# Input weights of the retention mixer in long runs, the first unit in four transfers, and products of ones at the seam

## The chip, the cores and the metric

One core of one Trainium2 chip runs the whole program. The metric is device microseconds of one execution, the median of several. The core has a matrix engine (PE, its weight loads shown as PEld), a vector engine (DVE), a scalar engine (ACT), GpSimd (POOL) and a sync engine (SP) that issues nearly all transfers here; 16 DMA engines carry them.

## The reference, cut to what matters

Two layers over 256 tokens of width 1024, all in float32. Each layer adds a mixer and then a mixture of experts (32 experts in 4 groups, two chosen per token). The first layer's mixer is attention, the second one's is retention. The work around the change is the end of the first layer's experts and the start of the retention mixer:

```
x = x + hier_moe(rmsnorm(x))              # layer 0, experts
z = rmsnorm(x) @ w_in_o                   # 1024 -> 6144: q, k (4 heads x 256), v, g (4 heads x 512)
q, k, v, g = split(z);  q, k = rope(q), rope(k)
o = rms(retention(q, k, v)) * silu(g)
x = x + o @ w_out_o
x = x + hier_moe(rmsnorm(x))              # layer 1, experts
```

## The kernel before, in words

Weights pass through a ring of 11 slots in SBUF, each 128 partitions by 4096 floats (2 MB, a "unit"). An experts' layer reads 96 units (gate, up and down of 32 experts), each of which lies in DRAM as one run of 16 KB per partition. The last of the 96 comes in two halves. SP issues all unit loads from one program in a fixed order; ahead of a load it waits until the slot's earlier unit is used (`moe_used`, `odd_used`).

The retention mixer reads 16 units in the order `ODD_ORDER`: for the first head qk, v and g, then qk, output weights, v and g of the next heads. `load_odd(j)` issues them. A qk unit is gathered from `w_in_o` by two transfers (q columns, k columns) in runs of 256 floats (1 KB), a v or g unit by one transfer in runs of 512 floats (2 KB); an output unit has longer runs. SP's order at the seam is: qk of head 0 into slot 6, the constants of the mixer (1 MB, `consts_odd`, runs of 8 KB per partition), v of head 0, g of head 0, qk of head 1, then three units of the next experts' layer.

Products with these weights run as three products of rounded parts. ACT writes the high part of a quarter of a unit (`high`, called through `odd_high_of`, L1316), DVE subtracts it to get the low part (`low`, through `odd_low_of`, L1639), and PE waits for the quarter's low part. At the seam ACT alternates: a quarter of the first unit, then two eighths of x (`high_x`, L1506); DVE follows with the low parts (L1639, L1925). ACT waits once for the whole first unit, ahead of its first quarter:

```
here = sum(32 if ODD_ORDER[n][0] == "qk" else 16 for n in range(j % 4, j + 1, 4))
act.wait_ge(odd_here[s_], here)
```

PE's order there is: the last combining products of the experts (`combine_last`, L1050); `first_qk`, 96 products of 256 columns (L1184), eight groups of 12, which needs quarter k // 2 and the low part of eighth k of x; `token_major("v", 0, row_squares)`, 24 products of 512 columns for the first 128 tokens (L657, L660, L661), then `row_squares` (L673) and 24 for the other tokens; `ret_scores` (L1211). `row_squares` takes the sums of squares of x. These are made by ACT (four squares, L1556, behind the four high quarters of v) and added by POOL (`sum_squares`, L627 three times and L628). DVE's order after the first unit is: low parts of v (L1639), the rotation of q and k (L1943, L1944, L1948, L1949, `rotate`), low parts of g, and then the row scales (L1991, L1992) that ACT needs to drain v (L1525). The second score product needs the PSUM bank that the first v occupied.

The routing, the experts and the retention stage are ordered by semaphores alone, nothing in them depends on absolute time.

Of the kernel before, what the change touches and what calls it, by code (L numbers as in the profile page):

```python
# [29 lines left out]
P = 128  # L30
SEQ = 256
TC = SEQ // P
D = 1024
DC = D // P
EPS = 1e-6
Q_LORA, KV_LORA, ROPE, NOPE, VD = 256, 128, 32, 64, 64
HEADS = 8
# [5 lines left out]
RH, RQK, RV = 4, 256, 512  # L43
# [5 lines left out]
UNIT = 4096  # L49
# [72 lines left out]


def build(nc, x_in, w_in_e, ln_q_e, w_uq_e, ln_kv_e, w_ukv_e, w_out_e,
          w_in_o, w_out_o, w_gate, w_up, w_down, ln_f, gains_turned, w_router, b_small, consts, consts_odd, out):
    ctx = ExitStack()
    with ctx:
        def sb(name, shape, dt=F32):
# [2 lines left out]
        def sem(name):  # L131
            return ctx.enter_context(nc.semaphore(name))
# [12 lines left out]
        def at(floats, name, shape, dt=F32):  # L145
            return nc.alloc_sbuf_tensor_at(name, shape, dt, offset=base + 4 * floats)[tuple(slice(None) for _ in shape)]

        ring = at(0, "ring", [P, RING, UNIT])
# [25 lines left out]
        x = at(4 * UNIT + 2048, "x", [P, TC, D])  # L174
# [64 lines left out]
        ones = cut(1)  # L239
        all_ones = ones.broadcast_to([P, P])  # L240
# [29 lines left out]
        gmax, first, sg4, p1 = (rt[:, 2 * k:2 * k + 2] for k in range(4))  # L270
# [18 lines left out]
        wk = [ctx.enter_context(nc.psum_tensor(f"wk{i}", [P, 512], F32)) for i in range(4)]  # L289
# [13 lines left out]
        odd_here = [sem(f"odd_slot{s}_loaded") for s in range(RING)]  # L303
        moe_used = [sem(f"moe{l}_units_used") for l in range(2)]
        odd_used = sem("odd_units_used")
        even_high, even_low = sem("even_high_parts"), sem("even_low_parts")
        odd_high, odd_low = sem("odd_high_parts"), sem("odd_low_parts")
        pe_s = sem("pe_steps")
# [78 lines left out]
        def wide(s):  # L387
            return ring[:, s, :].rearrange("p (c n) -> p c n", c=DC)

        def tall(s):  # L390
            return ring[:, s, :].rearrange("p (c n) -> p c n", c=4)
# [16 lines left out]
        def odd_parts(j):  # L408
            return ODD_HIGH[j % 2], ODD_RAW[j % 4]
# [16 lines left out]
        def last_unit(l, slot):  # L426
            return max(u for u in range(MOE_UNITS) if moe_slot(l, u) == slot)

        def unit_used(u):

            return RING + u + 1 - MOE_UNITS
# [3 lines left out]
        ODD_ORDER = [("qk", 0), ("v", 0), ("g", 0)]  # L435
# [29 lines left out]
        def _(sp):  # L465
# [17 lines left out]
            wo = w_out_e[0].rearrange("(u c p) n -> u p c n", u=2, c=4)  # L483
# [39 lines left out]
                load_expert_part(0, u)  # L523
            n0 = rest_of_experts(0)

            wi = w_in_o[0].rearrange("(c p) n -> p c n", p=P)
            wo2 = w_out_o[0].rearrange("(h c p) n -> h p c n", h=RH, c=4)

            def load_odd(j):
                kind, h = ODD_ORDER[j]  # L530
                s = odd_parts(j)[1]
                if kind == "qk":
                    for m in range(2):
                        sp.dma_start(wide(s)[:, :, m * RQK:(m + 1) * RQK],
                                     wi[:, :, h * RQK + m * RH * RQK:(h + m * RH + 1) * RQK]
                                     ).then_inc(odd_here[s], 16)
                elif kind == "wo":
                    sp.dma_start(tall(s), wo2[h]).then_inc(odd_here[s], 16)
                else:
                    first = 2 * RH * RQK + (RH * RV if kind == "g" else 0)  # L540
                    sp.dma_start(wide(s), wi[:, :, h * RV + first:(h + 1) * RV + first]).then_inc(odd_here[s], 16)

            def moe0_left(slot):
                sp.wait_ge(moe_used[0], n0 * MOE_UNITS + unit_used(last_unit(0, slot)))
# [2 lines left out]
            for j in range(4):  # L547

                moe0_left(odd_parts(j)[1])
                load_odd(j)  # L550
                if j == 0:
                    moe0_left(9)
                    sp.dma_start(odd[:, :], consts_odd).then_inc(odd_in, 16)
# [3 lines left out]
            for j in range(4, ODD_UNITS):  # L557

                sp.wait_ge(odd_used, 2 + j - 3)
                load_odd(j)  # L560
# [78 lines left out]
        def _(pe):  # L639
# [70 lines left out]
            for c in range(TC):  # L710
                last = nc.tensor.matmul(acc[3][:, tok(c)], rstd[:, c:c + 1].broadcast_to([P, P]), ident,
                                        start=True, stop=True)
# [21 lines left out]
            for c in range(TC):  # L734
                last = nc.tensor.matmul(wk[1][64:96, SEQ + c * P:SEQ + (c + 1) * P], zc[:, c, FQ - ROPE:FQ], ident,
                                        start=True, stop=True)
# [8 lines left out]
            for c in range(TC):  # L745
                for i, name in enumerate(("QA", "QB")):
# [4 lines left out]
                    b = wk[banks[f"{name}{c}"]]  # L751
# [6 lines left out]
            for m in range(4):  # L758
                pe.wait_ge(act_s, A.at(kn_free[m]))
                for i in range(2):  # L760
                    h = 2 * m + i
# [11 lines left out]
            for m in range(4):  # L773
# [8 lines left out]
                for i in range(2):  # L782
                    h = 2 * m + i
# [354 lines left out]
                        combine(1) if i < GROUPS - 1 else combine_last()  # L1138

            experts(0)  # L1140


            pe.sem_inc(odd_used, 2)
# [123 lines left out]
        def _(act):  # L1267
# [42 lines left out]
            def high(u_slot, h_slot, n, first, done, pieces=2, which=None):  # L1310

                for i in range(pieces) if which is None else (which,):
                    if i == 0:
                        first()
                    cols = slice(i * n // pieces, (i + 1) * n // pieces)
                    nc.scalar.activation(part[h_slot][:, cols], ring[:, u_slot, cols], ACT.Copy).then_inc(done, 1)  # L1316
# [170 lines left out]
            nr0, _ = experts(0, lambda b: act.wait_ge(pe_s, PE.at(f"OUT0:{b}")))  # L1487


            def odd_high_of(j, which=None):  # L1490
                h_slot, s_ = odd_parts(j)

                def first():

                    here = sum(32 if ODD_ORDER[n][0] == "qk" else 16 for n in range(j % 4, j + 1, 4))
                    act.wait_ge(odd_here[s_], here)
                    if j < 2:
                        act.wait_ge(moe_used[0], nr0 * MOE_UNITS + unit_used(last_unit(0, h_slot)))
                    else:
                        act.wait_ge(odd_used, j + 1)  # L1500
                high(s_, h_slot, UNIT, first, odd_high, 4, which)

            def high_x(j):
                if j % 2 == 0:
                    act.wait_ge(M[0][f"bank{j // 2}"], nr0)
                nc.scalar.activation(xh[:, j, :], turned_total[j], ACT.Copy, scale=gains[:, 2, j:j + 1]  # L1506
                                     ).then_inc(act_s, A.done(f"mix1:xh{j}"))

            for b in range(4):
                act.sem_inc(odd_drained[b], 1)  # L1510
            for n in range(4):
                odd_high_of(0, n)
                high_x(2 * n)
                high_x(2 * n + 1)

            def got(name, hp):
                b, k = odd_use(name, hp)
                act.wait_ge(odd_filled[b], (k + 1))
                return wk[b], odd_drained[b]
# [38 lines left out]
            b, d = got("ss", 0)  # L1558
# [9 lines left out]
            for h in range(RH):  # L1568
# [3 lines left out]
                if h < RH - 1:  # L1572
# [7 lines left out]
                    else:  # L1580
# [4 lines left out]
                        odd_high_of(4 * h + 7)  # L1585
            preload(ACT.Sqrt)
            _, summed = experts(1, lambda b: act.wait_ge(O[f"out{b}"], RH))
            def arrived(c):
                summed(c)
# [439 lines left out]
                   ).then_inc(dve_s, V.done(f"fin:xn{c}"))  # L2029


_INS = ['x', 'w_in_e', 'ln_q_e', 'w_uq_e', 'ln_kv_e', 'w_ukv_e', 'w_out_e', 'w_in_o', 'w_out_o', 'w_gate', 'w_up',
        'w_down', 'ln_f']


def turned(inputs):

    gains = np.stack([inputs["ln_mix_e"][0], inputs["ln_ffn"][0], inputs["ln_mix_o"][0], inputs["ln_ffn"][1]])
    gains = np.asarray(gains).reshape(4, DC, P).transpose(2, 0, 1).reshape(P, 4 * DC)
    w = np.concatenate([inputs["w_rg"], inputs["w_re"]], axis=2)  # L2040
    w = np.asarray(w).reshape(2, DC, P, NR).transpose(2, 0, 1, 3).reshape(P, 2 * DC * NR)
    b = np.concatenate([inputs["b_rg"], inputs["b_re"]], axis=1).reshape(1, 2 * NR)
    return [("gains_turned", gains), ("w_router", w),
            ("b_small", np.concatenate([b, np.asarray(inputs["b_f_e"]).reshape(1, HEADS)], axis=1))]


# [14 lines left out]
```

## Time and profile before

| | us |
|---|---|
| median of 3 runs | 1248.2 (1246.91 to 1249.69) |
| profiled execution, its own time | 1247.95 |
| its span in the trace | 1246.1 |
| PE busy | 947.9 (76%) |
| DVE, ACT busy | 332.3, 278.8 |
| moved from DRAM | 453.5 MB, 365 GB/s over the span |
| mean granted PE clock | 0.897 of full |

The page cuts the span in 40 slices. The first slices are the attention mixer, slices 5 to 18 the first experts, slices 19 to 25 the retention mixer, the rest the second experts and the final norm. A digit is a busy share in tenths; the times in a chain or timeline are microseconds from the span's start.

### The profile page before, as it was taken

The numbers are of one execution on the slowest core, as the hardware profiler recorded it, in microseconds if no ns is written. First come the engines' busy times: TensorE is split into PE (matmuls) and PEld (weight loads), VectorE is DVE, ScalarE is ACT, GpSimd is POOL, SyncE is SP. The second block draws the span as 40 slices with busy tenths as digits, with TensorE's granted clock in tenths as the row PEclk, the third lists the DMA queues.
The fourth block names the chain that finished last, engine by engine and source line by source line (L and its number), as shares of the span: only waits on it lengthen the run. The fifth ranks groups of instructions, "written<-read, shape, count | busy, mean of one in ns | idle before, by whom it ended". The sixth has DMA issues, their size and how long they took to land.

```text
span 1246.1 us, 29213 instructions
## 1 busy us (share of the span) xinstructions
PE 947.9 (76%) x13260; PEld 741.2 (59%) x13260; DVE 332.3 (27%) x713; ACT 278.8 (22%) x545; POOL 45.4 (4%) x68
## 2 busy tenths in 40 slices
PE   9999878767576665766999999968856575756665
PEld 6878756545354544544898988845634454435443
DVE  3666412111110111113664654312101111111112
ACT  5654411000000000003644445501100000000002
POOL 1043100000000000000100000100000000000000
PEclk9999899868798888788999999999989788889778
DMA  9456899999999999999954543999999999999995
GB/s 343 164 208 265 333 426 424 426 427 427 425 426 427 427 425 426 427 426 362 403 188 173 181 158 141 414 427 426 424 425 427 426 427 426 427 426 426 427 425 244
DMA packets 54862, 456.45 MB, mean 366 GB/s; under 512 B 4801, under 2 KB 14161, under 8 KB 29777
## 3 DMA queue, kind: packets, MB, share of 16 engines
q1 hardware_dynamic: 54512, 454.01, 88.3%
q8 instruction: 105, 1.72, 0.6%
q0 software_dynamic: 224, 0.55, 0.2%
q14 instruction: 21, 0.16, 0.0%
HBM read 453.50 MB, written 1.05 MB: 365 GB/s over the span
## 4 chain that ended last, share of the span: by engine, by line
PE 45%; DMA 45%; another core or an unknown queue 3%; DVE 3%; issue 2%; ACT 1%; POOL 1%; SPq 0%; DVEq 0%; PEldq 0%; POOLq 0%; ACTq 0%
DMA ring<-in_w_down 18%; DMA ring<-in_w_gate 16%; PE wk L1099 9%; DMA ring<-in_w_up 8%; PE wk L1132 5%; PE wk L657 4%; PE wk L661 4%; DMA ring<-in_w_in_o 4%; PE wk L660 4%; PE wk L1083 3%; PE total L657 2%; PE total L661 2%; PE total L660 2%; PE total L1027 1%
## 5 line engine op out<-in xcount | busy, mean ns | idle before, releaser
L1099 PE MATMUL wk<-ring,xg 128*32 128x128 f32 x8192 | 302.2, 309 | 157.3 <-DMA ring<-in_w_up 80.2
L1099 PEld LDWEIGHTS wk<-ring,xg 128*32 128x32 f32 x8192 | 259.6, 124 | 208.6 <-DMA ring<-in_w_up 92.2
L1132 PE MATMUL wk<-ring,hidT 128*32 128x256 f32 x2048 | 162.2, 469 | 108.5 <-DMA ring<-in_w_down 80.3
L1132 PEld LDWEIGHTS wk<-ring,hidT 128*32 128x32 f32 x2048 | 72.9, 129 | 181.4 <-issue 160.1
L1888 DVE TENSOR_TENSOR hid<-wk,act_g 128x128 f32<-128x128 f32 x64 | 24.0, 375 | 423.6 <-ACT act_g L1468 423.6
L1468 ACT ACTIVATE act_g<-wk 128x128 f32<-128x128 f32 x64 | 17.7, 277 | 451.6 <-PE wk L1099 451.6
L1482 ACT ACTIVATE ye<-wk 32x256 f32<-32x256 f32 x124 | 46.2, 373 | 280.4 <-PE wk L1132 279.7
L1902 DVE COPY ye<-wk 32x256 f32<-32x256 f32 x124 | 52.6, 424 | 205.0 <-PE wk L1132 204.2
L1639 DVE TENSOR_TENSOR slot_parts<-ring,slot_parts 128x1024 fp32r<-128x1024 f32 (+1 forms) x82 | 98.2, 1245 | 26.2 <-ACT slot_parts L1316 25.8
L1316 ACT ACTIVATE slot_parts<-ring 128x1024 fp32r<-128x1024 f32 (+1 forms) x82 | 83.0, 1069 | 39.5 <-PE wk L657 21.5
L1083 PEld LDWEIGHTS wk<-sel,scaled_rows 128*128 128x128 f32 x512 | 60.2, 195 | 11.7 <-issue 9.3
L1083 PE MATMUL wk<-sel,scaled_rows 128*128 128x128 f32 x512 | 62.1, 280 | 3.9 <-PE wk L1132 2.5
L657 PE MATMUL wk<-slot_parts,x_high 128*128 128x512 f32 x128 | 52.8, 412 | 0.6 <-DVE rotated_b L1944 0.6
L661 PE MATMUL wk<-slot_parts,x_low 128*128 128x512 f32 x128 | 50.5, 395 | 0.0
L660 PE MATMUL wk<-slot_parts,x_high 128*128 128x512 f32 x128 | 50.4, 394 | 0.0
L1020 PE MATMUL total<-gT,ye 128*128 128x256 f32 (+1 forms) x128 | 32.7, 411 | 3.2 <-DVE ye L1902 3.2
L1027 PE MATMUL total<-ye,gT 128*128 128x512 f32 (+1 forms) x64 | 29.9, 607 | 3.2 <-DVE ye L1902 3.2
L1020 PEld LDWEIGHTS total<-gT,ye 128*128 128x128 f32 (+1 forms) x128 | 25.5, 205 | 10.2 <-issue 6.7
L1877 DVE COPY xg<-wk 128x512 f32<-128x512 f32 x16 | 11.1, 691 | 71.8 <-PE wk L1083 71.8
L657 PEld LDWEIGHTS wk<-slot_parts,x_high 128*128 128x128 f32 x128 | 24.1, 188 | 6.8 <-issue 1.0
L599 POOL TENSOR_SCALAR xn<-xn,small 128x128 f32<-128x128 f32 (+1 forms) x32 | 24.9, 789 | 82.1 <-DVE small L1734 79.9
L660 PEld LDWEIGHTS wk<-slot_parts,x_high 128*128 128x128 f32 x128 | 24.1, 188 | 6.1 <-issue 1.0
(304 smaller groups left out, 1159.0 us busy)
## 6 DMA issues: line engine op xcount, KB each, us to landing
ring<-in_w_gate SPq DMA_DIRECT2D x64, 2048.0 KB, 49.0
ring<-in_w_up SPq DMA_DIRECT2D x64, 2048.0 KB, 49.7
ring<-in_w_down SPq DMA_DIRECT2D x62, 2048.0 KB, 49.1
ring<-in_w_in_o SPq DMA_DIRECT2D x8, 2048.0 KB, 8.6
ring<-in_w_in_o SPq DMA_DIRECT2D x8, 1024.0 KB, 11.4
ring<-in_w_out_o SPq DMA_DIRECT2D x4, 2048.0 KB, 8.3
ring<-in_w_in_e SPq DMA_DIRECT2D x3, 2048.0 KB, 17.2
ring<-in_w_out_e SPq DMA_DIRECT2D x2, 2048.0 KB, 12.3
```

The costliest lines, as they stand in the source:

```text
L657: ins = nc.tensor.matmul(dst, sh, mh, start=(k == 0 and first), stop=False, skip_group_check=True)
L660: nc.tensor.matmul(dst, sh, ml, start=False, stop=False, skip_group_check=True)
L661: last = nc.tensor.matmul(dst, sl, mh, start=False, stop=(k == n - 1 and last_one), skip_group_check=True)
L1020: last = nc.tensor.matmul(turned_total[j], ye[rows, j * P:(j + 1) * P], gT[rows, :], start=False, stop=False, skip_group_check=True)
L1027: last = nc.tensor.matmul(acc[2 * c + hf][:, :], gT[rows, tok(c)], ye[rows, hf * 512:(hf + 1) * 512], start=False, stop=False, skip_group_ ...
L1083: last = nc.tensor.matmul(b[:, k * P:(k + 1) * P], rows[:, c, 4 * half + k, :], sel[:, c, 4 * quad:4 * quad + 4, :].rearrange("p e s -> p ...
L1099: last = nc.tensor.matmul(wk[0][32 * j:32 * j + 32, part * P:(part + 1) * P], xe[:, k, :], w_[:, k, j * P:(j + 1) * P], start=(k == 0), st ...
L1132: last = nc.tensor.matmul(wk[3][32 * j:32 * j + 32, 0:256], hidT[:, k, :], wd[:, k, j * 256:(j + 1) * 256], start=(k == 0), stop=(k == 3))
L1316: nc.scalar.activation(part[h_slot][:, cols], ring[:, u_slot, cols], ACT.Copy).then_inc(done, 1)
L1482: last = nc.scalar.activation(ye[q, j * 256:(j + 1) * 256], wk[3][32 * j:32 * j + 32, 0:256], ACT.Copy)
L1639: tt(part[u_slot][:, cols], ring[:, u_slot, cols], part[h_slot][:, cols].bitcast(F32), ALU.subtract).then_inc(done, 1)
L1902: last = nc.vector.tensor_copy(ye[q, j * 256:(j + 1) * 256], wk[3][32 * j:32 * j + 32, 0:256])
```

## The change

1. The launch passes `w_in_o` no longer. It passes `units_o`, 12 units of 128 x 4096 floats, with each unit's row for a partition contiguous, in the order in which the ring's slot holds it (q and k columns of a head interleaved per 128-row block for qk). A load of such a unit is one transfer of 16 KB per partition. This is done on the host.
2. The first unit (qk of head 0) is loaded in four transfers, each a quarter of every partition's row (4 KB), with a semaphore for each. ACT waits for quarter n ahead of the high part of quarter n, no longer for the whole unit ahead of the first.
3. Behind the experts of the first layer PE issues five products of ones by ones, 128 x 128 by 256 columns, into a bank (`wk[3]`) that is free.

```
-                if kind == "qk":
-                    for m in range(2):
-                        sp.dma_start(wide(s)[:, :, m * RQK:(m + 1) * RQK],
-                                     wi[:, :, h * RQK + m * RH * RQK:(h + m * RH + 1) * RQK]
-                                     ).then_inc(odd_here[s], 16)
-                elif kind == "wo":
+                if kind == "wo":
                     sp.dma_start(tall(s), wo2[h]).then_inc(odd_here[s], 16)
+                elif j:
+                    sp.dma_start(ring[:, s, :], units_o["qk v g".split().index(kind) * RH + h]).then_inc(odd_here[s], 16)
                 else:
-                    first = 2 * RH * RQK + (RH * RV if kind == "g" else 0)
-                    sp.dma_start(wide(s), wi[:, :, h * RV + first:(h + 1) * RV + first]).then_inc(odd_here[s], 16)
+                    for n in range(4):
+                        quarter = slice(n * UNIT // 4, (n + 1) * UNIT // 4)
+                        sp.dma_start(ring[:, s, quarter], units_o[0][:, quarter]).then_inc(first_here[n], 16)
...
             experts(0)
+            for _ in range(5):
+                nc.tensor.matmul(wk[3][:, 0:SEQ], all_ones, ones.broadcast_to([P, SEQ]), start=True, stop=True)
...
-                    here = sum(32 if ODD_ORDER[n][0] == "qk" else 16 for n in range(j % 4, j + 1, 4))
-                    act.wait_ge(odd_here[s_], here)
+                    if j == 0:
+                        act.wait_ge(first_here[0], 16)
+                    else:
+                        act.wait_ge(odd_here[s_], 16 * len([n for n in range(j % 4, j + 1, 4) if n]))
...
             for n in range(4):
+                if n:
+                    act.wait_ge(first_here[n], 16)
                 odd_high_of(0, n)
                 high_x(2 * n)
                 high_x(2 * n + 1)
...
+    wo = np.asarray(inputs["w_in_o"])[0].reshape(DC, P, -1).transpose(1, 0, 2)
+    qk = [np.concatenate([wo[:, :, h * RQK:(h + 1) * RQK], wo[:, :, (RH + h) * RQK:(RH + h + 1) * RQK]], axis=2)
+          for h in range(RH)]
+    vg = [[wo[:, :, 2 * RH * RQK + (RH * m + h) * RV:2 * RH * RQK + (RH * m + h + 1) * RV] for h in range(RH)]
+          for m in range(2)]
+    units_o = np.stack([a.reshape(P, UNIT) for a in qk + vg[0] + vg[1]])
```

## Rows read from the trace of the kernel before

**Rows 1.** The chain that ended last, around the seam: start us, us, what.

```profile
539.24 43.84 DMA ring<-in_w_in_o
583.19 1.06 ACT slot_parts L1316
...
586.16 13.26 PE wk L1184 x96
```

**Rows 2.** Timeline of PE and PEld at the seam: start, us, line, count [idle before <-releaser].

```profile
536.77 1.95 PE L1099 MATMUL wk<-ring,xg 128*32 128x128 f32 x64 [1.54 <-DMA ring<-in_w_gate]
...
577.62 0.59 PEld L1132 LDWEIGHTS wk<-ring,hidT 128*32 128x32 f32 x16 [0.62 <-DMA ring<-in_w_down]
...
579.32 1.15 PE L1050 MATMUL total<-g_last,y_last 32*128 32x256 f32 x16 [0.63 <-DVE y_last L1899]
...
591.01 0.40 PE L1184 MATMUL wk<-x_high,slot_parts 128*128 128x256 f32 x2
...
591.37 0.40 PE L1184 MATMUL wk<-x_high,slot_parts 128*128 128x256 f32 x2
...
599.26 0.40 PE L657 MATMUL wk<-slot_parts,x_high 128*128 128x512 f32 x1
...
604.84 0.50 PE L673 MATMUL wk<-small,squares_odd 128*128 128x1 f32 x4
...
610.87 1.47 PE L1211 MATMUL wk<-qT,kT 128*128 128x256 f32 x8
```

**Rows 3.** Timeline of ACT at the seam.

```profile
578.76 0.38 ACT L1478 ACTIVATE y_last<-wk 64x256 f32<-64x256 f32 x1 [2.34 <-PE wk L1132]
591.18 3.91 ACT L1316 ACTIVATE slot_parts<-ring 128x1024 fp32r<-128x1024 f32 x4 [1.19 <-DMA ring<-in_w_in_o]
```

**Rows 4.** Stretches: us, busy of PE, PEld, DVE, ACT, POOL, PEclk, DMA share, GB/s.

```profile
35.00:37.00 2.00, 2.00 (x19) 2.00 (x19) 1.74 (x1) 1.96 (x3) 0.00 (x0) 1.00 1.03 411
596.00:598.00 2.00, 2.00 (x20) 2.00 (x19) 0.90 (x1) 1.02 (x3) 1.87 (x1) 1.00 1.07 349
860.00:1200.00 340.00, 220.80 (x4060) 158.08 (x4051) 47.77 (x120) 28.12 (x78) 0.00 (x0) 0.87 1.01 426
570.00:573.00 3.00, 2.41 (x28) 1.84 (x28) 0.42 (x1) 0.00 (x0) 0.00 (x0) 1.00 0.63 244
```

**Rows 5.** Timeline of SP's issues at the seam: start, us in the issue, transfer.

```profile
530.67 4.24 SPq L500 DMA_DIRECT2D ring<-in_w_down  x1
536.37 36.19 SPq L534 DMA_DIRECT2D ring<-in_w_in_o  x2
```

**Rows 6.** A timeline row of PE at the kernel's start: six products of ones.

```profile
9.52 2.78 PE L690 MATMUL total<-small 128*128 128x256 f32 x12
```

**Rows 7.** Stretches again, for the clock around waits and for the seam.

```profile
584.00:589.00 5.00, 2.84 (x13) 2.87 (x14) 4.69 (x7) 5.00 (x10) 0.00 (x0) 0.50 1.05 390
536.00:540.00 4.00, 1.95 (x64) 1.69 (x64) 0.15 (x1) 0.13 (x1) 0.00 (x0) 1.00 0.99 416
```

**Rows 8.** Timeline of POOL and DVE beside each other.

```profile
596.13 4.67 POOL L627 TENSOR_TENSOR squares_odd<-squares_odd 128x512 f32<-128x512 f32 x3 [450.51 <-ACT squares_odd L1556]
600.88 0.81 POOL L628 TENSOR_TENSOR squares_odd<-squares_odd 128x256 f32<-128x256 f32 x1
...
598.82 0.69 DVE L1943 TENSOR_TENSOR rotated_a<-wk,odd_consts 128x512 f32<-128x512 f32 x1 [1.93 <-PE wk L1184]
...
601.01 0.96 DVE L1949 TENSOR_TENSOR qT<-rotated_b,rotated_a 128x256 f32<-128x256 f32 x1
...
603.74 0.42 DVE L1949 TENSOR_TENSOR kT<-rotated_b,rotated_a 128x256 f32<-128x256 f32 x1
```

**Rows 9.** ACT's drain of the first v, in its timeline.

```profile
609.18 0.69 ACT L1525 ACTIVATE vr<-wk,small 128x512 f32<-128x512 f32 x1 [1.95 <-DVE small L1992]
```

**Rows 10.** Waits of ACT for a transfer, 580 to 800: total, times, longest.

```profile
ACT slot_parts L1316 <- DMA ring<-in_w_in_o: 5.2, 2, 4.0
```

**Rows 11.** A stretch of the retention mixer.

```profile
660.00:775.00 115.00, 114.41 (x675) 98.70 (x675) 62.65 (x82) 59.91 (x76) 0.00 (x0) 1.00 0.47 165
```

More of the change, by code:

```diff
@@ L124, in build @@
 def build(nc, x_in, w_in_e, ln_q_e, w_uq_e, ln_kv_e, w_ukv_e, w_out_e,
-          w_in_o, w_out_o, w_gate, w_up, w_down, ln_f, gains_turned, w_router, b_small, consts, consts_odd, out):
+          w_out_o, w_gate, w_up, w_down, ln_f, gains_turned, w_router, b_small, units_o, consts, consts_odd, out):
     ctx = ExitStack()
@@ L305, in build @@
         odd_used = sem("odd_units_used")
+        first_here = [sem(f"odd_first_quarter{n}_loaded") for n in range(4)]
         even_high, even_low = sem("even_high_parts"), sem("even_low_parts")
@@ L524, in _ @@
             n0 = rest_of_experts(0)
-            wi = w_in_o[0].rearrange("(c p) n -> p c n", p=P)
             wo2 = w_out_o[0].rearrange("(h c p) n -> h p c n", h=RH, c=4)
@@ L2029, in _ @@
                    ).then_inc(dve_s, V.done(f"fin:xn{c}"))
-_INS = ['x', 'w_in_e', 'ln_q_e', 'w_uq_e', 'ln_kv_e', 'w_ukv_e', 'w_out_e', 'w_in_o', 'w_out_o', 'w_gate', 'w_up',
+_INS = ['x', 'w_in_e', 'ln_q_e', 'w_uq_e', 'ln_kv_e', 'w_ukv_e', 'w_out_e', 'w_out_o', 'w_gate', 'w_up',
         'w_down', 'ln_f']
@@ L2042, in turned @@
     b = np.concatenate([inputs["b_rg"], inputs["b_re"]], axis=1).reshape(1, 2 * NR)
+    wo = np.asarray(inputs["w_in_o"])[0].reshape(DC, P, -1).transpose(1, 0, 2)
[4 more added lines that the diff above has]
+    units_o = np.stack([a.reshape(P, UNIT) for a in qk + vg[0] + vg[1]])
     return [("gains_turned", gains), ("w_router", w),
-            ("b_small", np.concatenate([b, np.asarray(inputs["b_f_e"]).reshape(1, HEADS)], axis=1))]
+            ("b_small", np.concatenate([b, np.asarray(inputs["b_f_e"]).reshape(1, HEADS)], axis=1)), ("units_o", units_o)]
 def kernel(**inputs):
```

## The prediction, made before the changed kernel ran

> **What bounds the kernel now.** I read the chain of waits first. At the seam it steps from the experts to the landing of the mixer's first unit at 583.08 (539.24 + 43.84), and from there over ACT and DVE to the 96 products of `first_qk` at 586.16 [rows 1]. So the seam is set by a landing, not by an engine: the last combining products start at 579.32 and are over at 580.47, ACT's last copy of the experts ends at 579.14 [rows 2, 3], and both then wait. Next I read the stretches. While PE waits its clock falls from 1.0 to 0.5, and the first 3.8 us of `first_qk` run at half clock [rows 7]. From there to the next experts PE has no wait worth a microsecond: 114.41 of 115.00 us busy at clock 1.0 [rows 11]. The second experts are bound by transfers, 426 GB/s at a share of 1.01 [rows 4], but their loads are released by PE's progress through the retention stage (each slot must be used first), so what PE gains at the seam and keeps through the mixer moves all that follows. A loading time inside the mixer is worth nothing: from 580 to 800 ACT waits for a transfer twice only, 4.0 us for the first unit and 1.2 for the first v [rows 10, 3].
>
> **The first unit.** In the trace the last experts' half unit is at hand at 577.6 (PEld waits 0.62 us for it) [rows 2], the first unit at 583.08: 5.46 us for 2.10 MB. In runs of 1 KB the core moves 349 GB/s, in 4 KB 411, in 16 KB 426 [rows 4]. A quarter in runs of 4 KB is 0.524 MB, 1.28 us at 411 GB/s. The quarters then land at 578.9, 580.2, 581.5 and 582.7. ACT wants the first at 579.14, so it starts at about 579.2 in place of 583.19, 4.0 us earlier. It has three instructions for a quarter (one for it, two for eighths of x), ten of them in 5.00 us with no gap [rows 7], some 1.6 us for each quarter, and wants the others at 580.8, 582.4 and 584.0: each is there, with 0.6 us or more to spare. Were one late, what is queued behind it on ACT is `high_x` and, through DVE, PE; even with these three 0.6 us later nothing moves. The first low part is ready for PE 2.97 us after ACT's start (583.19 to 586.16) [rows 1]: at 582.2.
>
> A rule speaks against any gain from the layout: the Trainium skill (DMA: Bandwidth & Descriptors, Specifications) gives 512 B as the smallest transfer for line rate, by which 1 KB runs would be as fast as 16 KB. The trace does not agree: 349 against 426 GB/s [rows 4]. By the rule the first v would not come earlier, which is the second rival below.
>
> **SP.** Its two issues of the first unit take 36.19 us [rows 5]. At 570 to 573 a part of the DMA engines has run dry (share 0.63) while others still carry the last expert unit [rows 4]. With long runs SP has four issues in place of two. I bound each by the 4.24 us that an expert unit's issue took [rows 5] and by nothing: at worst they end at 553.4, and constants, v, g and the next qk follow by 570. So nothing waits for an issue. The dry engines get work, but the last expert unit's landing is that of the other engines; I count nothing for it (bounds: none, to 0.6 us, the whole of PEld's wait for it).
>
> **Products of ones.** They start when the combining ends, at 580.5. Six such products took 2.78 us at full clock [rows 6], 0.463 each, so five end at 582.8. That is 0.6 us past the 582.2 at which the real ones could start. `first_qk` therefore starts at 582.8, 3.3 us earlier than before. What they buy is the clock: PE has no longer a gap of 5.7 us (580.47 to 586.16) that brought 0.5 [rows 7]. At full clock three products take 0.36 us (591.01 to 591.37, 0.118 each) [rows 2]; 96 take 11.4 in place of 13.26, another 1.9 us. DVE keeps ahead: its three steps for a quarter are 2.0 us (seven in 4.69) [rows 7], PE's 24 products 2.8. So the first product of v, before at 599.26 [rows 2], comes at about 594.1, 5.1 us earlier.
>
> **What is late next.** Two chains hang on the first v and do not move by 5.1 us.
> - The v unit. Before, 3.15 MB (constants and v) took from 583.08 to 591.18, where ACT starts [rows 3]: about 8.0 us. With v in 16 KB runs I take 426 GB/s, 7.4 us, behind a last quarter at 582.7: 590.1, ACT at 590.2, 1.0 us earlier. PE wants its low part at 594.1; with the first unit high, low and an eighth of x took 2.97 us from ACT's start, so it is done by 593.2. No stall there.
> - The squares. They stand behind v's high parts on ACT, then POOL adds them from 596.13 to 601.69 [rows 8]. PE wanted them at 604.84 [rows 2] and had 3.1 us to spare. Now POOL starts at 595.1 and ends at 600.7, while PE's 24 products (5.58 us, 599.26 to 604.84) are over at 599.7. The spare time is used up and PE waits 1.0 us.
> - Beside this POOL now meets DVE's rotation, which before had waited 1.93 us for PE and will follow the low parts at once. Where they met before, a DVE step of two SBUF operands took 0.96 us where its twin took 0.42 [rows 8]. I add 0.4 us to POOL (bounds 0 and 0.9: none or two of these 0.54 us stretches, less what overlaps). POOL ends at 601.1, PE waits 1.4.
> - DVE's chain to the row scales starts 1.0 us earlier and loses its 1.93 us wait: 2.9 in all, less some 0.5 of such meetings. ACT's drain of the first v then starts at 606.7 in place of 609.18 [rows 9] and ends at 607.4.
>
> The Trainium skill (SBUF — State Buffer, Who interferes with whom) says that a DVE instruction with two SBUF inputs and a GpSimd instruction that reads SBUF exclude each other for a whole instruction. The stretched row agrees. By the rule every one of POOL's four steps could meet one DVE step of 0.42 us, and the sum would be up to 1.3 us smaller.
>
> From the squares the rest is as before: `row_squares` to the scores took 604.84 to 610.87, 6.03 us [rows 2]. 601.1 + 6.03 = 607.1: 3.7 us earlier. The second score, 0.65 us later at 607.8, finds its bank drained at 607.4. From there on all engines' work, and the loads that PE releases, moves by 3.7 us.
>
> **The sum.** Start of `first_qk` 3.3, clock 1.9 (together 5.1, rounded), less the new wait for the squares 1.4: 3.7 us. On the profiled execution, 1247.95 - 3.7 = 1244.2; its median is 0.25 us higher, so 1244.5. The edit of the other eleven units beyond the first v is worth nothing, hidden by PE's products; were that cover gone, each would bring 0.4 to 1.1 us (2.10 MB at 426 GB/s against 393, which 3.15 MB in 8.0 us come to, or 349). Cases inside the forecast: squares reach POOL with no meeting (gain 4.1), with the full one (3.2); clock not held (then v's products begin at 596.0 and end at 601.6, gain 3.2); v no earlier (2.7). That these fall together at 3 to 4 is because the squares' chain caps the gain, whatever PE does.
>
> **Rivals.**
> 1. The squares do not bind: the first v lands 1 us sooner than I think, since dry DMA engines get work. PE's whole 5.1 us come through: 1243.1. For it: the share of 0.63. Against: the landing waits for the slowest engine. 0.10.
> 2. Long runs gain no rate: the first v lands at 591.1 as before, POOL ends at 602.1 or, with a longer meeting, 602.6; gain 2.3 to 2.7: 1245.7. 0.14.
> 3. The quarters land together. The four lie in one queue of 16 engines; if the landing of the first also waits for engines that lag by several microseconds, ACT starts at 582 and the gain is 1 to 1.5 us: 1247.0. For it: engines do finish at different times here (0.63). Against: the lag ends with the last expert half, which is at hand at 577.6. 0.12.
> 4. PE's clock falls at the new wait. A wait of 1.54 us ahead of 536.77 left it at 1.0 [rows 2, 7], 5.7 us brought 0.5; 1.4 us lies below both. If it falls, 6.8 us at half clock (583.1 to 589.9 before) cost up to 3.4: 1247.9. 0.04.
> 5. Slower than before: the replacement of one input by another moves where the expert weights lie in DRAM, and the second experts move less than 426 GB/s. They take 201 MB, 472 us at this rate; 0.8% eats the 3.7 us, 1.3% gives 1250.7. For it: the stage is bound by nothing else. Against: 426 stands in both experts' layers, from different places. 0.07.
>
> The forecast has 0.53. The range leaves out the tail beyond rival 1, rival 4 and rival 5: 1242.9 to 1247.3. A measurement of this kernel can tell about 0.2%, 2.5 us, from no change. Faster by more: the forecast, rival 1 and half of rival 2, 0.70. Within: the other half, rivals 3 and 4, 0.23. Slower: rival 5, 0.07.
>
> **What would show it.** Right: ACT's first quarter (L1316) near 579.2; the ones between 580.5 and 582.8; L1184 starting at 582.8 with clock 1.0 throughout and 11.4 us long; a wait of PE for POOL at L673 of 1 to 2 us; L1211 near 607.1; all later rows 3.7 us earlier and 426 GB/s in the experts. Wrong: ACT still waiting past 580 for the first quarter, a clock of 0.5 behind 583, no wait at L673, or a shift at L1211 that the end of the span does not show.

## The result, and the profile after

The changed kernel runs in 1245.7 us (median of 20, 1243.31 to 1248.19) against 1248.26 for the kernel before on the same chips. The ratio is 0.9975, 95% interval 0.9968 to 0.9982. I go by the ratio: 3.1 us faster, 2.2 to 4.0 (the two medians lie 2.6 us apart). The forecast was 3.7 us and 1244.5, and the time lies in its range, 1242.9 to 1247.3. It is also the time that the second rival gave (1245.7, the first v no earlier), so the time can't tell the two apart. The trace does.

The one profiled execution took 1248.04 us with a span of 1246.2, as long as the one before (1247.95, 1246.1). It is 2.3 us above the median, and the end of this section shows where it lost what the seam gained. Its busy line from the page:

```profile
PE 945.1 (76%) x13270; PEld 739.7 (59%) x13270; DVE 333.7 (27%) x713; ACT 278.5 (22%) x545; POOL 45.5 (4%) x68
```

Its experts end 0.44 us later than before (the combining products start at 579.76, at 579.32 in [rows 2]), so I count from this start. PE's timeline at the seam, which answers [rows 2]; L1048 is the combining, L1140 the products of ones, L1184 `first_qk`, L655 the first product of v, L671 `row_squares`, L1211 the scores, L1221 the first retention product:

```profile
579.76 1.15 PE L1048 MATMUL total<-g_last,y_last 32*128 32x256 f32 x16 [0.63 <-DVE y_last L1903]
581.46 2.43 PE L1140 MATMUL wk<-small 128*128 128x256 f32 x10 [0.55 <-PE total L1048]
583.54 0.47 PE L1184 MATMUL wk<-x_high,slot_parts 128*128 128x256 f32 x1
...
595.03 0.40 PE L655 MATMUL wk<-slot_parts,x_high 128*128 128x512 f32 x1
...
601.47 0.58 PE L671 MATMUL wk<-small,squares_odd 128*128 128x1 f32 x4 [0.71 <-POOL squares_odd L626]
...
607.57 1.85 PE L1211 MATMUL wk<-qT,kT 128*128 128x256 f32 x8
...
614.84 1.02 PE L1221 MATMUL wk<-vr,sT 128*128 128x512 f32 x2
```

The first retention product of the kernel before, which [rows 2] lack:

```profile
617.75 1.02 PE L1221 MATMUL wk<-vr,sT 128*128 128x512 f32 x2
```

`first_qk` starts 3.78 us from the combining (6.84 before), the first product of v 15.27 (19.94), the scores 27.81 (31.55), and the first retention product 35.08; before it started at 617.75, 38.43. So the seam gained 3.06, 4.67, 3.74 and in the end 3.35 us. The eight score products are 1.85 us long and not 1.47: a wait hides between the fourth and the fifth. The chain of waits names it (start, us, what):

```profile
563.34 27.33 DMA ring<-in_units_o
590.76 1.07 ACT slot_parts L1316
...
597.89 1.34 issue
599.23 1.53 DVE qT L1953
...
602.97 4.63 DVE slot_parts L1643 x4
607.71 0.17 DVE small L1996
607.97 0.70 ACT vr L1529
608.71 0.71 PE wk L1211 x4
```

It now runs from the landing of the first v through DVE: low parts of v, rotation, low parts of g, row scales, then ACT's drain of v, whose bank the second score product wants. ACT's timeline of the changed kernel, for [rows 3]:

```profile
579.72 1.06 ACT L1316 ACTIVATE slot_parts<-ring 128x1024 fp32r<-128x1024 f32 x1
...
590.76 3.91 ACT L1316 ACTIVATE slot_parts<-ring 128x1024 fp32r<-128x1024 f32 x4 [3.98 <-DMA ring<-in_units_o]
```

DVE's, and then POOL's, for [rows 8]. The kernel before first, with a row that [rows 8] lack, then the changed one:

```profile
600.21 0.87 DVE L1948 TENSOR_TENSOR qT<-rotated_a,rotated_b 128x256 f32<-128x256 f32 x1
```

```profile
597.79 1.51 DVE L1952 TENSOR_TENSOR qT<-rotated_a,rotated_b 128x256 f32<-128x256 f32 x1
599.23 1.52 DVE L1953 TENSOR_TENSOR qT<-rotated_b,rotated_a 128x256 f32<-128x256 f32 x1
...
602.51 0.42 DVE L1953 TENSOR_TENSOR kT<-rotated_b,rotated_a 128x256 f32<-128x256 f32 x1
```

```profile
595.71 4.75 POOL L625 TENSOR_TENSOR squares_odd<-squares_odd 128x512 f32<-128x512 f32 x3 [449.39 <-ACT squares_odd L1560]
```

And SP's queue, for [rows 5]:

```profile
537.07 21.27 SPq L539 DMA_DIRECT2D ring<-in_units_o  x4
```

ACT starts on the first quarter with no wait for a transfer. By the landings in the trace the four quarters are there at 579.30, 580.58, 581.82 and 583.28, and ACT starts on them at 579.72, 581.65, 583.31 and 584.97. The first was only 0.3 us ahead of ACT's last copy, and the last came 3.5 us after the combining, hardly sooner than the whole unit did in the kernel before (3.8). Two rotation steps are 1.5 us long where their twins take 0.42: they stand beside POOL's sums. Before, the same two took 0.87 and 0.96. SP's four issues take 21.27 us where the two took 36.19.

The stretches of the changed kernel (columns as in [rows 4]): the DMA engines no longer run dry at 570 to 573, PE's clock is 1.0 at 584 to 589, and the second experts run at 426 GB/s as before. But at 789.5 to 795 the clock is 0.5 (1.0 before), and at 800 to 810 the transfers fall behind (419 GB/s before).

```profile
570.00:573.00 3.00, 2.47 (x29) 1.72 (x20) 0.42 (x1) 0.00 (x0) 0.00 (x0) 1.00 1.01 406
584.00:589.00 5.00, 5.00 (x45) 5.00 (x44) 4.70 (x9) 2.78 (x6) 0.00 (x0) 1.00 1.03 437
789.50:795.00 5.50, 5.50 (x27) 5.50 (x28) 2.77 (x18) 2.25 (x4) 0.00 (x0) 0.50 1.01 432
800.00:810.00 10.00, 8.50 (x170) 7.67 (x173) 2.52 (x8) 3.85 (x6) 1.44 (x6) 1.00 0.92 356
860.00:1200.00 340.00, 222.56 (x4104) 159.37 (x4092) 47.79 (x120) 28.12 (x78) 0.00 (x0) 0.86 1.01 426
```

That is the routing ahead of the second experts. From ACT's first squares (L1430) to the first gather (L1081) it took 22.58 us; in the kernel before, at clock 1.0, 780.36 to 800.91, 20.55. So 2.9 us of gain went in and 0.9 came out. From the gather to the end of the span it is another 1.0 us more than before (446.2 against 445.2; in the ten profiles of this document this stretch lies between 443.9 and 446.3). First the two rows of the kernel before, then those of the changed one:

```profile
780.36 0.60 ACT L1430 ACTIVATE squares<-total 128x512 f32<-128x512 f32 x1 [6.46 <-PE total L661]
...
800.91 3.84 PE L1083 MATMUL wk<-sel,scaled_rows 128*128 128x128 f32 x32 [0.70 <-DVEq L1860]
```

```profile
777.45 0.60 ACT L1430 ACTIVATE squares<-total 128x512 f32<-128x512 f32 x1 [6.46 <-PE total L659]
```

```profile
800.03 3.84 PE L1081 MATMUL wk<-sel,scaled_rows 128*128 128x128 f32 x32 [0.70 <-DVEq L1864]
```

### The profile page after: what moved, and what is told of

Its sections match the earlier page's. It is cut to its first block, busy times and chain, and to the rows that moved or that the text cites. A ratio compares the mean times of both kernels' runs of the same rounds, so it can differ in the third digit from the quotient of the medians.

```text
span 1246.2 us, 29232 instructions
## 1 busy us (share of the span) xinstructions
PE 945.1 (76%) x13270; PEld 739.7 (59%) x13270; DVE 333.7 (27%) x713; ACT 278.5 (22%) x545; POOL 45.5 (4%) x68
## 4 chain that ended last, share of the span: by engine, by line
DMA 44%; PE 44%; another core or an unknown queue 4%; DVE 3%; issue 2%; ACT 1%; POOL 1%; SPq 0%; DVEq 0%; PEldq 0%; ACTq 0%; POOLq 0%
DMA ring<-in_w_down 21%; DMA ring<-in_w_gate 12%; PE wk L1097 9%; DMA ring<-in_w_up 8%; PE wk L1130 5%; PE wk L655 3%; PE wk L659 3%; PE wk L658 3%; PE wk L1081 3%; DMA ring<-in_units_o 2%; PE total L655 2%; PE total L659 2%; PE total L658 2%; PE total L1025 1%
## 5 line engine op out<-in xcount | busy, mean ns | idle before, releaser
L1097 PE MATMUL wk<-ring,xg 128*32 128x128 f32 x8192 | 296.4, 306 | 158.5 <-DMA ring<-in_w_up 83.3
L1097 PEld LDWEIGHTS wk<-ring,xg 128*32 128x32 f32 x8192 | 255.6, 123 | 208.8 <-DMA ring<-in_w_up 95.1
L1081 PEld LDWEIGHTS wk<-sel,scaled_rows 128*128 128x128 f32 x512 | 60.3, 196 | 11.7 <-issue 9.4
L1081 PE MATMUL wk<-sel,scaled_rows 128*128 128x128 f32 x512 | 62.2, 281 | 4.0 <-PE wk L1130 2.6
L655 PE MATMUL wk<-slot_parts,x_high 128*128 128x512 f32 x128 | 52.8, 412 | 0.6 <-DVE rotated_b L1948 0.6
L1018 PE MATMUL total<-gT,ye 128*128 128x256 f32 (+1 forms) x128 | 30.0, 386 | 3.2 <-DVE ye L1906 3.2
L655 PEld LDWEIGHTS wk<-slot_parts,x_high 128*128 128x128 f32 x128 | 24.1, 188 | 6.8 <-issue 1.0
```

Source lines behind the costliest of these rows:

```text
L655: ins = nc.tensor.matmul(dst, sh, mh, start=(k == 0 and first), stop=False, skip_group_check=True)
L1018: last = nc.tensor.matmul(turned_total[j], ye[rows, j * P:(j + 1) * P], gT[rows, :], start=False, stop=False, skip_group_check=True)
L1081: last = nc.tensor.matmul(b[:, k * P:(k + 1) * P], rows[:, c, 4 * half + k, :], sel[:, c, 4 * quad:4 * quad + 4, :].rearrange("p e s -> p ...
L1097: last = nc.tensor.matmul(wk[0][32 * j:32 * j + 32, part * P:(part + 1) * P], xe[:, k, :], w_[:, k, j * P:(j + 1) * P], start=(k == 0), st ...
```

## The experiments

Theory: the four own waits are the gain. Products of ones add nothing at this point, the layout brings the v unit about a microsecond earlier, and chains behind v cap what PE gains. Rivals: the clock (so the ones), or the layout and the DMA engines that had run dry. The table has, from each one's trace, microseconds from the start of the combining products to the start of `first_qk`, of the first product of v, of ACT's high parts of v, of `row_squares`, of the scores, and of the first retention product. The last column is the timed ratio to the kernel before, timed beside it. One us is 0.0008 of it, so most single steps are read from the traces, of which each kernel has one.

| kernel | first_qk | v product | ACT on v | row_squares | scores | retention | ratio (95%) |
|---|---|---|---|---|---|---|---|
| before | 6.84 | 19.94 | 11.86 | 25.52 | 31.55 | 38.43 | |
| changed | 3.78 | 15.27 | 11.00 | 21.71 | 27.81 | 35.08 | 0.9975 (0.9968 to 0.9982) |
| e1, ones only | 6.86 | 19.77 | 11.88 | 25.35 | 31.38 | 38.26 | 1.0000 (0.9989 to 1.0012) |
| e2, layout only | 6.24 | 19.88 | 10.61 | 25.46 | 31.48 | 38.36 | 1.0002 (0.9991 to 1.0013) |
| e3, quarters only | 2.94 | 15.87 | 12.22 | 22.93 | 29.03 | 36.28 | 0.9979 (0.9970 to 0.9989) |
| e4, without ones | 2.93 | 14.31 | 11.04 | 21.72 | 27.81 | 35.09 | 0.9974 (0.9963 to 0.9985) |
| e5, scales first | 3.78 | 15.27 | 10.44 | 21.16 | 27.27 | 34.15 | 0.9971 (0.9961 to 0.9981) |
| e6, squares first | 3.78 | 15.27 | 10.90 | 20.84 | 26.86 | 35.11 | 0.9975 (0.9964 to 0.9987) |
| e7, both first | 3.77 | 15.27 | 10.90 | 20.83 | 26.85 | 33.73 | 0.9959 (0.9947 to 0.9972) |
| e9, both, no ones | 2.93 | 14.32 | 10.90 | 20.76 | 26.77 | 33.65 | 0.9954 (0.9939 to 0.9970) |

**The ones alone (e1).** Into the kernel before:

```
             experts(0)
+            for _ in range(5):
+                nc.tensor.matmul(wk[3][:, 0:SEQ], all_ones, ones.broadcast_to([P, SEQ]), start=True, stop=True)
```

> The kernel before with the five products of ones behind the first experts; the weights' layout and the single wait as before. Theory (a wait for the landing, then a clock that fell): first_qk still starts 2.97 us after the landing, but is 11.4 us long in place of 13.26, and the squares' 3.1 us of spare time cover that, so from the start of the combining products (579.32 before) to the first retention product (617.75 before) it takes 36.5 us in place of 38.43: 1.9 us less. Rival (the ones end some 2.3 us ahead of the first real product, and the clock falls in that gap all the same): first_qk 13.26 us long, 38.4 us, nothing gained.

The rival was right. PE's timeline and a stretch:

```profile
581.77 2.43 PE L1142 MATMUL wk<-small 128*128 128x256 f32 x10 [0.55 <-PE total L1050]
586.94 0.41 PE L1186 MATMUL wk<-x_high,slot_parts 128*128 128x256 f32 x1 [2.74 <-DVE x_low L1927]
```

```profile
587.50:590.00 2.50, 2.50 (x14) 2.50 (x13) 2.50 (x4) 2.50 (x5) 0.00 (x0) 0.50 1.04 384
```

PE still idles for 2.74 us behind the ones, and the clock falls at 587.1, just after the real products start. Before it fell at 583.1. Now it stays down for 3.4 us in place of 6.8. The gain is 0.17 us.

**The layout alone (e2).** The changed kernel without the ones, with one transfer and one wait:

```
-                elif j:
+                else:
                     sp.dma_start(ring[:, s, :], units_o["qk v g".split().index(kind) * RH + h]).then_inc(odd_here[s], 16)
-                else:
-                    for n in range(4):
...
-                    if j == 0:
-                        act.wait_ge(first_here[0], 16)
-                    else:
-                        act.wait_ge(odd_here[s_], 16 * len([n for n in range(j % 4, j + 1, 4) if n]))
+                    act.wait_ge(odd_here[s_], 16 * len(range(j % 4, j + 1, 4)))
...
-                if n:
-                    act.wait_ge(first_here[n], 16)
```

> The changed kernel with the first unit in one transfer of 16 KB runs and one wait, and without the products of ones. Theory (the layout alone hardly shortens the first unit, whose landing is set by the last expert unit ahead of it): ACT starts 4.0 to 4.3 us after the end of its last copy of the experts (4.05 before), first_qk begins at half clock; 38.2 us from the combining products to the first retention product, 0 to 0.4 us less than before. The last quarter of the changed kernel, which lands at the same place in the queue, says the same. Rival (DMA engines that ran dry before are the gain): at least 1.5 us less.

As the theory said, 0.07 us. ACT's wait for the unit is 3.45 us, a little under the expected 4.0, and v is at hand 1.25 us earlier. But `first_qk`, 0.60 us earlier, starts into a clock of 0.5 and is longer by nearly as much (13.64 us to the first product of v, 13.10 before), and nobody waited for v.

**The quarters alone, in the old short runs (e3).** Into the kernel before, with the waits of the changed kernel (32 for each quarter):

```
+                if j == 0:
+                    for n in range(4):
+                        for m in range(2):
+                            sp.dma_start(wide(s)[:, 2 * n:2 * n + 2, m * RQK:(m + 1) * RQK],
+                                         wi[:, 2 * n:2 * n + 2, m * RH * RQK:(m * RH + 1) * RQK]
+                                         ).then_inc(first_here[n], 16)
```

> The kernel before with the first unit in quarters with own waits, each of two transfers in the old 1 KB runs, without the products of ones. Theory (the quarters' own waits are the gain, and the squares' chain behind the v unit caps it): ACT starts within 0.3 us of the end of its last copy, first_qk some 3.9 us earlier, PE idle under 2 us so the clock stays at 1.0; v lands as before, PE waits for POOL at row_squares; 36.0 to 36.6 us from the combining products to the first retention product, 1.9 to 2.4 us less than before. Rival (short runs and SP's long issues hold back the later quarters): ACT waits between the quarters, under 1.2 us less.

2.15 us of the 3.35, as expected, with no wait between the quarters though SP sat 39.60 us in these eight issues. Against the expectation the clock did fall, 1.3 us after `first_qk` had started behind a gap of 1.79 us. It didn't matter: v is at hand no earlier than before (12.22, 11.86 before), and PE waits for POOL.

```profile
581.59 0.36 PE L1191 MATMUL wk<-x_high,slot_parts 128*128 128x256 f32 x1 [1.79 <-DVE x_low L1937]
...
601.58 0.58 PE L680 MATMUL wk<-small,squares_odd 128*128 128x1 f32 x4 [1.33 <-POOL squares_odd L635]
```

```profile
583.00:586.00 3.00, 3.00 (x16) 3.00 (x15) 3.00 (x6) 2.68 (x6) 0.00 (x0) 0.50 1.04 394
```

Its time (0.9979) can't be told from that of the changed kernel: that the layout adds the other 1.2 us rests on the traces of e3 and e4.

**Without the ones (e4).** The changed kernel, with the two lines of e1 taken out.

> The changed kernel without the products of ones. Theory (the chains behind v cap the gain, so neither the ones nor their 0.9 us past the point where the first weights are ready cost or bring anything): first_qk starts 0.7 to 0.9 us earlier than in the changed kernel (relative to the combining products), clock 1.0 or a fall, and in both cases 35.0 to 35.4 us to the first retention product (35.08 in the changed kernel). Rival (the ones are what holds the clock and so a good part of the gain): first_qk at half clock and at least 1 us more.

`first_qk` starts 0.85 us earlier and the end is the same to 0.01 us. The ones neither cost nor brought anything; all went into the wait for the sums:

```profile
582.66 0.35 PE L1182 MATMUL wk<-x_high,slot_parts 128*128 128x256 f32 x1 [1.79 <-DVE x_low L1927]
...
601.45 0.58 PE L671 MATMUL wk<-small,squares_odd 128*128 128x1 f32 x4 [1.67 <-POOL squares_odd L626]
```

The clock stayed at 1.0 here after the same gap of 1.79 us, and once more in e9 below. So a gap of this length goes either way.

```profile
583.00:586.00 3.00, 3.00 (x28) 3.00 (x27) 3.00 (x5) 3.00 (x7) 0.00 (x0) 1.00 1.01 429
```

**The row scales first (e5).** In DVE's order of the changed kernel:

```
             rotate(0)
-            odd_low_of(2)
             dve.wait_ge(act_s, A.at("mix1:std"))
             link(nc.vector.reciprocal(row_r, std))
             tt(row_r2, row_r, row_r, ALU.mult).then_inc(dve_s, V.done("mix1:rs"))
             dve.wait_ge(dve_s, V.at("mix1:rs"))
+            odd_low_of(2)
```

> The changed kernel with DVE's two row-scale instructions moved ahead of the low parts of the first g unit (they stood behind). Theory (the second score product waits for the bank of the first v, whose drain waits for these scales, which are late because DVE's rotation meets POOL's sums): ACT drains v some 4.4 us earlier, the wait of the first g product goes, 34.6 to 34.8 us from the combining products to the first retention product (35.08 in the changed kernel), the two stretched rotation rows stay at 1.5 us. Rival (the wait for the sums alone caps the gain): 35.0 to 35.1.

The wait in the scores is gone (6.88 us from the scores to the first retention product, as before the change, 7.27 in the changed kernel). The sum, 34.15, is below what was expected because v was at hand 0.56 us sooner after the combining in this execution; counted from ACT's start on v it is 23.71 us against 24.08, 0.37 less. ACT's drain starts 4.7 us earlier than in the changed kernel (4.4 expected). The rotation steps stay at 1.51 and 1.52.

**The squares first (e6).** In ACT's order of the changed kernel:

```
-            odd_high_of(1)
             act.wait_ge(dve_s, V.at("mix1:xl7"))
             for b in range(4):
                 nc.scalar.activation(sq_odd[:, b, :], acc[b], ACT.Square).then_inc(act_s, A.done(f"mix1:sq{b}"))
+            odd_high_of(1)
```

> The changed kernel with ACT's four squares of x moved ahead of the high parts of the first v unit, into the 4 us in which ACT waits for that unit. Theory (the sums stood behind v's landing): PE's wait at row_squares goes (1.0 us from end to start), POOL's four sums run beside the low parts of v, so DVE's rows of the rotation fall from 1.5 back to 0.42 us and some of the rows of the low parts are stretched instead, by up to 1.3 us each; then the scales are next, 34.1 to 34.6 us from the combining products to the first retention product. Rival (squares ahead of v hold back v's high parts): PE waits in the products of v, 35 us or more.

The wait at `row_squares` went and the rotation is back at 0.43 us, but the sum missed its range: 35.11. What POOL held up moved with it. DVE's four low parts of v took 6.93 us in place of 4.63, POOL's last step 1.60 in place of 0.79, and the scales and ACT's drain were as late as ever. DVE's timeline of this kernel, then POOL's, then PE's:

```profile
592.13 6.93 DVE L1643 TENSOR_TENSOR slot_parts<-ring,slot_parts 128x1024 fp32r<-128x1024 f32 x4 [3.08 <-ACT slot_parts L1316]
...
600.35 0.43 DVE L1952 TENSOR_TENSOR qT<-rotated_a,rotated_b 128x256 f32<-128x256 f32 x1
```

```profile
595.23 1.60 POOL L626 TENSOR_TENSOR squares_odd<-squares_odd 128x256 f32<-128x256 f32 x1
```

```profile
609.08 0.71 PE L1211 MATMUL wk<-qT,kT 128*128 128x128 f32 x4 [1.09 <-ACT vr L1529]
```

**Both moves (e7).**

> Both moves in the changed kernel. Theory: neither wait is left, PE runs through from first_qk to the first retention product, 33.6 to 33.9 us from the combining products, 1.2 to 1.5 us less than the changed kernel, and the whole 4.7 to 4.8 us of the seam come through against the kernel before. Rival (a third chain behind v of nearly the same length): 34.2 or more.

33.73 us: no wait of PE from `first_qk` to the retention product. The seam's whole 4.70 us come through. By the ratio the kernel is 5.1 us faster than the one before (3.5 to 6.6), the lowest ratio of all kernels with the ones. Each move alone brought nothing that timing can tell from the changed kernel. The interval of both moves still overlaps that of the changed kernel (0.9972 against 0.9968), so that they add to it rests on the trace, 1.35 us, and on the medians timed beside it (1243.45, against 1246.23 for e5 and 1246.08 for e6).

```profile
594.79 0.40 PE L655 MATMUL wk<-slot_parts,x_high 128*128 128x512 f32 x1
...
600.35 0.50 PE L671 MATMUL wk<-small,squares_odd 128*128 128x1 f32 x4
...
606.37 1.47 PE L1211 MATMUL wk<-qT,kT 128*128 128x256 f32 x8
...
613.25 1.02 PE L1221 MATMUL wk<-vr,sT 128*128 128x512 f32 x2
```

**Both moves, no ones (e9).**

> Both moves and no products of ones. Theory (with the caps gone the ones are on the path, since they end 0.9 us past the point where the first low parts are ready): first_qk starts 2.9 us after the combining products in place of 3.8; if the clock stays at 1.0, 32.7 to 33.2 us to the first retention product; if it falls as in the kernel with quarters in short runs, first_qk is 12.9 us long and the sum is 33.9 to 34.8, no better than with the ones. Rival (the low parts of the first v are then late for PE): a wait in the products of v of up to 0.8 us at clock 1.0, 33.5.

The clock stayed, PE was 0.95 us earlier at the first product of v and then lost 0.87 us in these products, waiting for low parts: 33.65. Four of these parts take DVE 6.92 us beside POOL's sums, 4.63 without. The two versions can't be told apart by their times. What holds the low parts is no longer v's landing: it lands 10.47 us from the combining, and ACT starts on it at 10.90, with no wait, when its squares are done. So by the trace the next cap is the squares in front of v on ACT and the sums beside DVE's low parts; no run here takes these away.

```profile
591.59 3.92 ACT L1314 ACTIVATE slot_parts<-ring 128x1024 fp32r<-128x1024 f32 x4
...
592.70 6.92 DVE L1641 TENSOR_TENSOR slot_parts<-ring,slot_parts 128x1024 fp32r<-128x1024 f32 x4 [3.07 <-ACT slot_parts L1314]
...
596.87 0.50 PE L655 MATMUL wk<-slot_parts,x_high 128*128 128x512 f32 x1 [0.30 <-DVE slot_parts L1641]
```

## Why the prediction was right, step by step

The mechanism that caps the gain, a chain behind the first v, came out as forecast up to the scores. One more cap, which the prediction had priced and found in time, took 0.4 us of it.

- *The landing sets the seam, and quarters let ACT start 4.0 us earlier.* Right: ACT started 0.14 us after its last copy (579.58 to 579.72), and waited between none of the quarters. e3 shows that this part alone is 2.15 of the 3.35 us, e2 that without it there is nothing. The 582.2 for the first low part is right by luck: it was counted from ACT's start (2.97 us), but ACT's first part of x needs the combining products and started when they ended (580.92 and 580.91). PE then idles for 1.79 us behind them in e3, e4 and e9, and 580.47 + 1.79 happens to be 582.3.
- *`first_qk` 3.3 us earlier, clock 1.9 more, together 5.1.* A little off: 3.06 and 1.61. The ones started 0.55 us late, behind PE's wait for its own combining products, and took 0.2 less to the next start. 13.26 was the length to the last product's end, not to the next start (13.10). That they hold the clock: in the changed kernel it was held, but e4 held it without them, and e1 shows that ones with a longer gap behind them don't. For this kernel's time they are nothing.
- *The first v lands 1.0 us earlier.* Right, 0.86: by the landings 0.24 is the first unit's and 0.62 the faster stretch behind it (7.38 us for constants and v, 8.00 before; 7.4 forecast). It is what the layout is worth here: e3 without it is 1.2 us behind e4 at the retention product. With quarters v was at hand 11.0 us from the combining in long runs and 12.2 in short ones. One profile's figure can be off by half a microsecond: e5, with the same transfers as the changed kernel, has 10.44.
- *PE then waits for the sums of squares, scores 3.7 us earlier.* Right: 3.74. In it two misses cancel without mattering, since POOL's end sets the place: PE came later (4.67 for 5.1) and so waited less (0.9 us for 1.4). POOL's end moved by 0.80 us where 0.6 was forecast: its start gave 0.1 less, and of the 0.4 us that the prediction added for meetings POOL lost hardly any (4.75 us for its three sums, 4.67 before).
- *DVE's chain to the row scales ends in time.* Wrong, and the mis-sized term. I put 0.5 us on what DVE loses in its meetings with POOL over what it lost before. The two steps took 1.51 and 1.52 us, 0.87 and 0.96 before, so the loss is 1.2 us (2.2 in all over their own 0.42). Put the other way: ACT's drain of v started 1.65 us earlier, not 2.5. The drain was late by 0.4 us at the second score, so 3.74 became 3.35. The Trainium skill (SBUF — State Buffer, Who interferes with whom) says that a DVE instruction with two SBUF inputs contends with a GpSimd instruction that reads SBUF. The prediction set the rule's further cost on POOL, and DVE bore it. The rows agree with the rule, and e6 shows the meeting to be the cause by moving the sums away from the rotation: the stretch leaves these rows and appears in the low parts beside which the sums now run.
- *SP and the dry engines.* Right: the issues took 21 us, the engines stayed busy at 570 to 573, and nobody waited for an issue. e2 has busy engines too and gains 0.07 us at the retention product. How much of the first unit's 0.24 us comes of the fed engines and how much of the rate, no run separates.
- *From there all moves by the same amount.* Right on average, 3.1 us (2.2 to 4.0) for 3.35, but not in one execution. The routing ahead of the second experts has a second fall of PE's clock. Of ten profiled kernels eight show it at 788.8 to 792.7 (for 3.4 us: 20.96 to 21.05 us from ACT's squares to the gather; for 6.8: 22.58 to 22.59), among them e2, whose seam didn't move, and two don't, the kernel before and e1 (20.55, 20.56). These two are also the only ones with neither the new layout nor the quarters, so that the change brings the fall on isn't ruled out: each kernel has one profile. A loss of 2.0 us in every execution is: it would leave 1.35 us of the seam's 3.35, and the timed gain is at least 2.2. A loss of 0.4 us would fit the times.
- *Rivals.* 1, v's landing early enough to lift the cap: it came 0.86 us earlier, and PE waited. 2, v no earlier: the landing refutes it, not the time. 3, quarters that land together: they landed 1.2 to 1.5 us apart. 4, the clock at the new wait: 1.0 throughout, with 0.71 us idle. 5, the place of the inputs in DRAM: the experts move 426 GB/s before and after.

## What to carry to other kernels

When a stall at a landing goes, list every chain that starts at the next landing and its spare time before the change: here 3.1 us at the sums and 1.7 at the drain of v's bank (done at 609.18 + 0.69, wanted by the fifth score product at 610.87 + 0.74, half of the eight products' 1.47). These spare times, plus what each chain itself got earlier (0.8 us for POOL's end, 1.65 for the drain), and not the 4.7 us of the seam, set the gain. Two caps of nearly the same height hide each other: taking one away shows nothing in the times until the other goes too (e5 and e6 against e7). Parts of a change that come together should be run apart: the ones and the layout by themselves are worth nothing, the layout 1.2 us beside the quarters by the traces, and the ones nothing in company either. One profiled execution can hide a gain of 3 us, as it did here: count from a common start, stage by stage, and leave the sum to the timed runs.

## What the runs showed of the hardware

- A DVE step with two SBUF operands took 1.51 us beside POOL's sums, whose steps of 128 x 512 take 1.3 us, and 0.42 without them. Beside DVE's steps of 1.2 us POOL's last sum took 1.60 us (e6), 0.79 in the changed kernel.
- After an idle gap of 1.79 us PE's clock once fell to 0.5 (e3) and twice stayed (e4, e9). After 2.74 us behind products of ones (e1), 5.10 (e2) and 5.70 (before) it fell.
- SP's issues of the first unit took 36.19 us for 2 transfers in 1 KB runs, 39.60 for 8 of them (e3) and 21.27 for 4 in 4 KB runs, and nobody waited for any of them.
- A transfer doesn't land at once on all 16 DMA engines: of the last expert unit's second half, in the kernel before, eight had landed by 569.6 and the other eight came at 575.2 to 577.6, and its reader starts with the last.
